# Expert rows cut into four column quarters and transposed by VectorE; expert weights in 4 KB runs

## The reference, cut to what matters

```
u = rms_norm(x, norm2_g) * (1 + sc2) + sh2
gate = two experts of one group of four, for each token, weights summing to 1
for e in 16 experts:  y += gate[:, e] * ((silu(u @ w1[e]) * (u @ w3[e])) @ w2[e])
x = x + g2 * y
```

## Time and profile before

| | us |
|---|---|
| median of 3 runs | 792.46 (792.24 to 792.88) |
| the profiled execution | 785.36 |
| its span, first to last instruction | 783.4 |
| TensorE busy | 627.1 (80%) |
| VectorE busy | 324.8 (41%) |
| ScalarE busy | 248.4 (32%) |
| mean TensorE clock granted | 0.915 |

### The profile page before, as it was taken

The page is one execution under the profiler, slowest core; times in us unless marked ns, Lnnn a source line. Parts: engine busy times, 40 slices in busy tenths (PEclk is TensorE's granted clock), DMA queues, the critical chain, the costliest instruction groups (busy, mean ns, idle before and its releaser), DMA issues.

```text
span 783.4 us, 15541 instructions
## 1 busy us (share of the span) xinstructions
PE 627.1 (80%) x6206; PEld 377.8 (48%) x6210; DVE 324.8 (41%) x917; ACT 248.4 (32%) x605; POOL 78.1 (10%) x118
## 2 busy tenths in 40 slices
PE   0389999977688889779988059989999999999940
PEld 0354465565355566554448035555555555555520
DVE  2824326523177797962352412222222222222215
ACT  2010100104255575851141023334433344433410
POOL 4010000007100000000000400011101111101122
PEclk9869999988889999999995579999999999999985
DMA  8894743343299300019016446999999999999228
GB/s 293 331 346 165 267 161 145 124 130 96 96 344 220 120 1 1 2 41 387 2 60 262 182 160 224 366 366 364 374 365 362 370 366 368 373 363 361 86 57 298
DMA packets 78108, 176.25 MB, mean 225 GB/s; under 512 B 9202, under 2 KB 24122, under 8 KB 75002
## 3 DMA queue, kind: packets, MB, share of 16 engines
q1 hardware_dynamic: 65328, 152.90, 55.7%
q0 software_dynamic: 8384, 13.97, 5.3%
q10 hardware_dynamic: 4364, 8.94, 3.6%
HBM read 155.02 MB, written 20.71 MB: 224 GB/s over the span
## 4 chain that ended last, share of the span: by engine, by line
PE 26%; DMA 23%; DVE 2%; issue 2%; POOL 2%; ACTq 0%; ACT 0%; POOLq 0%
DMA featT<-expert_rows 21%; PE score L1451 9%; PE score L1371 7%; PE bank L1441 3%; PE score L1460 3%; PE score L1411 2%; DMA pool_sb<-expert_rows,idx 1%; POOL expert_rows L727 1%; POOL pool_sb L747 1%; DMA expert_rows<-pool_sb,idx 1%; DMA expert_rows<-featT 1%; PE bank L1466 0%; ACTq L623 0%; PE bank L1403 0%; PE bank L1319 0%
## 5 line engine op out<-in xcount | busy, mean ns | idle before, releaser
L1451 PE MATMUL score<-pool_sb,featT 128*32 128x256 f32 x2688 | 162.6, 386 | 20.0 <-DMA featT<-expert_rows 11.3
L1451 PEld LDWEIGHTS score<-pool_sb,featT 128*32 128x32 f32 x2688 | 86.6, 111 | 82.1 <-DMA featT<-expert_rows 27.1
L1199 PE MATMUL bank<-pool_sb,featT 128*128 128x512 f32 (+2 forms) x320 | 113.7, 518 | 2.9 <-DVE pool_sb L804 1.9
L1128 DVE TENSOR_TENSOR featT<-featT,score 128x128 f32<-128x128 f32 x42 | 12.1, 288 | 184.2 <-ACT featT L634 184.2
L1199 PEld LDWEIGHTS bank<-pool_sb,featT 128*128 128x128 f32 x320 | 61.4, 193 | 54.9 <-issue 49.0
L1460 PE MATMUL score<-pool_sb,featT 128*32 128x256 f32 x1344 | 82.3, 386 | 0.4 <-ACT featT L639 0.4
L628 ACT ACTIVATE featT<-bank,mod_col 128x32 f32<-128x32 f32 x129 | 39.4, 375 | 61.4 <-PE bank L1441 61.4
L777 DVE SCALAR_TENSOR_TENSOR pool_sb<-pool_sb,cond 128x2048 f32<-128x2048 f32 x24 | 56.3, 2348 | 3.3 <-DMA pool_sb<-in_ada_b 1.7
L1118 DVE TENSOR_SCALAR featT<-bank,mod_col 128x32 f32<-128x32 f32 x215 | 51.0, 303 | 15.1 <-PE bank L1441 15.1
L735 POOL DMA_DIRECT2D expert_rows<-featT x42 | 29.2, 695 | 277.6 <-DVE featT L1124 264.0
L1371 PE MATMUL score<-pool_sb,featT 128*128 128x512 f32 x128 | 55.6, 594 | 0.0
(11 more groups left out here) (232 smaller groups left out, 648.3 us busy)
## 6 DMA issues: line engine op xcount, KB each, us to landing
pool_sb<-in_moe_w SPq DMA_DIRECT2D x48, 2048.0 KB, 22.1
pool_sb<-in_ada_w SPq DMA_DIRECT2D x24, 1024.0 KB, 5.0
expert_rows<-zeros_f SPq DMA_DIRECT2D x17, 512.0 KB, 6.7
featT<-expert_rows ACTq DMA_DIRECT2D x44, 128.0 KB, 5.4
expert_rows<-featT POOLq DMA_DIRECT2D x42, 128.0 KB, 7.1
pool_sb<-in_w_in SPq DMA_DIRECT2D x2, 2048.0 KB, 9.1
pool_sb<-in_w_out SPq DMA_DIRECT2D x4, 1024.0 KB, 16.9
x_sb<-in_x SPq DMA_DIRECT2D x1, 2048.0 KB, 7.9
```

What stands on the lines that cost most here:

```text
L1199: m = nc.tensor.matmul(banks[4 + i][:, 0:n], featT[:, k, i * P:(i + 1) * P], w_stage[:, g % 3, k, 0:n], start=(k == 0), stop=(k == KD - 1))
L1451: mm = nc.tensor.matmul(banks[0][h * BT:(h + 1) * BT, 0:2 * HB], xgT[:, k, :], exp_w13[slot][:, :, k, h * HB:(h + 1) * HB], start=(k == 0) ...
```

## The change

- **Rows.** A block is loaded as 4 x 32 quarters of 1 KB, quarter h into partitions 32h to 32h + 31, into two buffers in turn (`xg[n]`), three blocks ahead. VectorE multiplies by `scale2_part` and adds `shift2_part` (both new, held in quarters as the gate is), which gives `xm`, and transposes that in squares of 32 x 32 into `xgT` in one instruction that reads every eighth element. The transposes of TensorE and the eight evictions are gone.
- **Hidden rows.** `hmid` is transposed the same way by VectorE into `hT`; the turn on TensorE and the copy on ScalarE are gone. ScalarE keeps only the silu and the issue of the row loads.
- **Order.** `inner` no longer waits for row loads; it waits for `xgT` of its own block and for `hmid` of the block before.
- **Weights.** Input row p x 8 + k (for w2, p x 4 + k) now lies in partition p, which fits the squares. Each matrix comes in four DMAs with runs of 4 KB per partition, 16 KB (w2 too) apart from one partition to the next.
- **Ahead of the stage.** TensorE makes shift, gate and scale of the second norm in quarters (4 matmuls of 32 x 256 more at the second group, 8 of these in place of 2 of 128 x 512 at the third); VectorE copies them; four small DMAs of `norm2_g` are added at the start.

```diff
@@ sp
-                sp.dma_start(chunk_of(e % 3, m, DE // P if m == 2 else KD),
-                             MOE_W[m][0, e].rearrange("(k p) n -> p k n", p=P)).then_inc(done, 16)
+                rows = DE // P if m == 2 else KD
+                to, of = chunk_of(e % 3, m, rows), MOE_W[m][0, e].rearrange("(p k) n -> p k n", p=P)
+                for q in range(4):
+                    part = slice(q * rows // 4, (q + 1) * rows // 4)
+                    sp.dma_start(to[:, part, :], of[:, part, :]).then_inc(done, 16)
@@ act
+            def xg_load(g, n):
+                act.dma_start(xg[n], xs[bass.ds(g * BT, BT), :].rearrange("r (h n) -> h r n", h=NT)).then_inc(s_xg[n], 16)
+
+            def block_of_rows(g, n):
+                act.wait_ge(m_sc, g + 2)
+                xg_load(g + 3, 1 - n)
                 act.wait_ge(m_h1, g + 1)
                 nc.scalar.activation(silu, banks[0][:, 0:HB], ACT.Silu).then_inc(m_si, 1)
-                act.wait_ge(m_xt, g + 2)
-                xg_load(g + 2)
-                xg_T(g + 1)
-                act.wait_ge(m_ht, g + 1)
-                nc.scalar.activation(hT, banks[6][:, 0:P], ACT.Copy).then_inc(m_hT, 1)
@@ dve
+                                nc.vector.tensor_copy(shift2_part[:], banks[3][:, 0:DN])
...
-                                for h in range(NT):
-                                    at0 = (h * DN) % 512
-                                    nc.vector.tensor_copy(gate2_part[h * BT:(h + 1) * BT, :],
-                                                          banks[h * DN // 512][h * BT:(h + 1) * BT, at0:at0 + DN])
+                                nc.vector.tensor_copy(gate2_part[:], banks[0][:, 0:DN])
+                                dve.wait_ge(s_n2, 16 * NT)
+                                nc.vector.scalar_tensor_tensor(out=scale2_part[:], in0=banks[1][:, 0:DN], scalar=1.0, in1=scale2_part[:],
+                                                               op0=ALU.add, op1=ALU.mult)
...
+            def rows_in(g, n):
+                dve.wait_ge(s_xg[n], g * 8 + (16 if n == 0 else 8))
+                if not (isinstance(g, int) and g == 0):
+                    dve.wait_ge(m_xT, g)
+                nc.vector.tensor_tensor(xm, xg[n], scale2_part[:], ALU.mult).then_inc(m_sc, 1)
+                dve.wait_ge(m_sc, g + 1)
+                nc.vector.tensor_tensor(xm, xm, shift2_part[:], ALU.add).then_inc(m_mod, 1)
+
             def xg_T(g):
+                dve.wait_ge(m_mod, g + 1)
+                nc.vector.transpose(xgT, xm.rearrange("p (r k) -> p k r", k=KD)).then_inc(m_xT, 1)
+
+            def hmid_T(g):
+                dve.wait_ge(m_h, g + 1)
+                nc.vector.transpose(hT, hmid.rearrange("p (r k) -> p k r", k=NT)).then_inc(m_hT, 1)
...
+            def hidden(g):
+                dve.wait_ge(m_h1, g + 1)
+                xg_T(g + 1)
                 dve.wait_ge(m_si, g + 1)
+                if not (isinstance(g, int) and g == 0):
+                    dve.wait_ge(m_hT, g)
                 nc.vector.tensor_tensor(hmid, silu, banks[0][:, HB:2 * HB], ALU.mult).then_inc(m_h, 1)
+
+            def block_of_rows(g, n, y):
+                hidden(g)
+                dve.wait_ge(m_y, g)
+                hmid_T(g)
+                rows_out(y)
+                rows_in(g + 2, n)
@@ pe
+            def inner(slot, g):
+                pe.wait_ge(m_xT, g + 1)
                 for k in range(KD):
-                    if k == KD - 1:
-                        pe.wait_ge(s_xg, g * 16 + 32)
...
             def stage_of(g, slot, slot_before, uses):
-                pe.wait_ge(e_w13[slot], uses * 32)
+                pe.wait_ge(e_w13[slot], uses * 128)
+                pe.wait_ge(m_h, g)
                 inner(slot, g)
-                xg_T()
-                pe.wait_ge(e_w2[slot], uses * 16)
+                pe.wait_ge(e_w2[slot], uses * 64)
                 outer(g - 1, slot_before)
-                inner_T(g)
```

More of the change, by code:

```diff
@@ L77, in decoder_layer @@
         gate2_part = sb("gate2_part", [P, DN])
+        scale2_part = sb("scale2_part", [P, DN])
+        shift2_part = sb("shift2_part", [P, DN])
         gate1_row = sb("gate1_row", [P, D])
@@ L179, in decoder_layer, with blk_view @@
         blkbuf = featT[:, :, :].rearrange("p k n -> p (k n)")
[L180 to L186, removed]
+        blk_at = [0]
+        def blk_view(n):
+            blk_at[0] += n
+            return blkbuf[:, blk_at[0] - n:blk_at[0]]
+        xg = [blk_view(DN) for _ in range(2)]
+        xm = blk_view(DN)
+        xgT = blk_view(DN).rearrange("p (k r) -> p k r", r=BT)
+        silu = blk_view(HB)
+        hmid = blk_view(HB)
+        hT = blk_view(HB).rearrange("p (k r) -> p k r", r=BT)
+        y_sb = [blk_view(DN) for _ in range(2)]
+        y_last = [blk_view(DN) for _ in range(2)]
         yab = ring[:, :, 0:TT * D].rearrange("p b (i n) -> p b i n", i=TT)
@@ L316, in decoder_layer @@
         s_scat = sem("s_scat")
-        s_xg = sem("s_xg")
+        s_n2 = sem("s_n2")
+        s_xg = [sem(f"s_xg{n}") for n in range(2)]
+        m_mod = sem("m_mod")
+        m_sc = sem("m_sc")
         m_h1 = sem("m_h1")
@@ L320, in decoder_layer @@
         m_h = sem("m_h")
[L321 to L324, removed]
+        m_xT = sem("m_xT")
         m_hT = sem("m_hT")
@@ L380, in _ @@
                 sp.dma_start(vrow[28:32, b * DH:(b + 1) * DH], beta_swa[0, half].rearrange("(i d) -> i d", d=DH)).then_inc(s_small, 16)
+            for h in range(NT):
+                sp.dma_start(scale2_part[h * BT:(h + 1) * BT, :], norm2_g[0:1, h * DN:(h + 1) * DN].broadcast_to([BT, DN])).then_inc(s_n2, 16)
             for n, pos in enumerate((cmp_pos_k, cmp_pos_v)):
@@ L435, in _ @@
             load_matrix(2, 2)
-            sp.wait_ge(s_xg, 32)
+            sp.wait_ge(s_xg[0], 16)
+            sp.wait_ge(s_xg[1], 16)
             load_matrix(2, 0)
@@ L1136, in _ @@
             for g in range(1, 3):
-                block_of_rows(g)
-                rows_out(y_sb[(g - 1) % 2], g)
+                block_of_rows(g, g % 2, y_sb[(g - 1) % 2])
             with dve.Fori(1, pairs - 1) as m:
[L1140 to L1144, removed]
-                rows_out(y_sb[1], m * 2 + 2)
-            block_of_rows(pairs * 2 - 1)
-            last = dve.value_load(block_start[0:1, NE + 2:NE + 3], min_val=MIN_BLOCKS * NE - 1, max_val=MAXB)
-            rows_out(y_last[0], last)
-            rows_out(y_last[1], last + 1)
+                for n in range(2):
+                    hidden(m * 2 + 1 + n)
+                    dve.wait_ge(m_y, m * 2 + 1 + n)
+                    hmid_T(m * 2 + 1 + n)
+                    dve.wait_ge(s_ys[n], m * 16)
+                    rows_out(y_sb[n])
+                    rows_in(m * 2 + 3 + n, 1 - n)
+            last = dve.value_load(block_start[0:1, NE + 2:NE + 3], min_val=MIN_BLOCKS * NE - 1, max_val=MAXB)
+            hidden(last)
+            dve.wait_ge(m_y, last)
+            hmid_T(last)
+            rows_out(y_last[0])
+            dve.wait_ge(m_y, last + 1)
+            rows_out(y_last[1])
             for i in range(TT):
@@ L1211, in _, with quarters @@
                     row, col = (0, 1024) if g == 2 else (1024, 0)
-                    for h in range(2):
-                        nc.tensor.matmul(banks[h][:], ones[:], acc[:, b, row + h * 512:row + (h + 1) * 512], start=True, stop=True)
+                    def quarters(to, at0):
+                        for h in range(NT):
+                            nc.tensor.matmul(to[h * BT:(h + 1) * BT, 0:DN], ones[:, 0:BT], acc[:, b, at0 + h * DN:at0 + (h + 1) * DN],
+                                             start=True, stop=True)
+                    if g == 2:
+                        for h in range(2):
+                            nc.tensor.matmul(banks[h][:], ones[:], acc[:, b, row + h * 512:row + (h + 1) * 512], start=True, stop=True)
+                        quarters(banks[3], col)
+                    else:
+                        quarters(banks[0], row)
+                        quarters(banks[1], col)
                     for k in range(8):
@@ L1436, in _ @@
             m.then_inc(r_rank, 1)
-            def xg_T():
+            def inner(slot, g):
+                pe.wait_ge(m_xT, g + 1)
                 for k in range(KD):
-                    at0 = (k % 5) * BT
-                    m = nc.tensor.transpose(banks[4 + k // 5][:, at0:at0 + BT], xg[:, k * P:(k + 1) * P], ident[0:BT, 0:BT])
-                m.then_inc(m_xt, 1)
-            def inner(slot, g):
-                pe.wait_ge(m_xa, g + 1)
-                pe.wait_ge(m_xv, g + 1)
-                for k in range(KD):
-                    if k == KD - 1:
-                        pe.wait_ge(s_xg, g * 16 + 32)
                     for h in range(NT):
@@ L1480, in expert @@
                     stage_of(g, slot, slot, uses)
[L1482 to L1484 removed]
+            pe.wait_ge(e_w13[0], 128)
             inner(0, 0)
[L1486 to L1487 removed]
             pe.wait_ge(t_gs, 1)
```

52 lines of the change are left out of this document (17 added, 35 removed).

## The result

The changed kernel takes **801.66 us** (median of 4 runs, 799.78 to 804.19) against 792.35 (787.88 to 792.88, 4 runs) for the kernel before, run beside it: 1.0132 times as long, 95% interval 1.0084 to 1.018 (all ratios here are worked out over all the runs, so that they differ a little from the quotient of the medians). The forecast was 762.5 us, with a range up to 785. The profiled execution took 804.19 us.

What follows compares the result with a forecast made beforehand. The loop through one row buffer was taken as the bound, with the weights next. 785.36 - 29.1 - 0.9 = 755.4 us for the profiled execution; 30.0 off the median gave 762.5 us, range 754 to 785.

Steps and rivals of the forecast that it cites:

- the row load: In the block loop: a load, wanted two blocks on, lands in 7.1 us like the store; hidden, with cover to 10.3 us.
- the rows bind again: Rival, block loop: four times as many pieces queue, loads land in about 12.8 us, block near 6.85, 785.5 us; chance 0.12 (rows or VectorE).
- The signs of being wrong that came: Set beforehand: engine time per MB not falling, a block inside an expert over 6.3 us, or TensorE waiting on VectorE.
- Block of TensorE: In the expert stage: inner of 3.66 us and outer of 1.93 us remain, 5.6 us a block, hiding VectorE's new work.
- VectorE's transposes: In each block: 0.56 us for the 128 x 256 transpose and 0.35 in VectorE's sum of 2.5 us, under 5.6.
- Weights at 6.12 us a matrix: Weight stream of the stage: 4 KB runs at 42.3 us per MB save 0.32 us a matrix, from 6.44 to 6.12.
- the first rival: Weight stream: longer runs buy nothing, a matrix stays at 6.44 us, 773.0 us in all; chance 0.13.
- the slower rival: Weight stream: 16 KB spacing costs more than the runs save; at 50 us per MB, 7.13 us a matrix, 799.0 us; chance 0.09.
- Start of the stream: Start of the stage: the third inner frees slot 0, so the weight stream starts at 473.5 and not at 476.21.
- The 0.9 us forecast as gain there: Ahead of the stage: third group 1.8 us less, second group 0.9 us more, sum -0.9 us, bounds +0.9 and -1.8.
- End of the last outer: End of the stage: TensorE waits last for the 33rd matrix at 675.5, then needs 49.5 us: 725.0, 29.1 before 754.1.

Runs made afterwards that it cites:

- c_q4: The changed kernel with each row load as four DMAs, one for each column quarter, instead of one; 760.93 us, ratio 0.9625 to the kernel before.
- f_few: `c_q4` plus, every second block behind the silu, an unread load of 32 rows of `x` in one DMA, quarters first; 798.09 us.
- c_q4_kp1: `c_q4` with the weights loaded as before the change (one DMA a matrix, 2 KB runs); 766.06 us, ratio 0.9701 to the kernel before.
- b_pk4: The kernel before with weights loaded as in the changed kernel (four DMAs, 4 KB runs); 786.14 us, ratio 0.9972.
- b_four: The kernel before with each matrix in four DMAs, same placement and runs; 789.39 us, ratio 0.9984.
- d_b_pre: The kernel before with only the change's part ahead of the stage (quarters of shift, gate, scale, their copies, four small DMAs); 789.71 us against 791.97.
- f_all: As `f_few`, but the unread load's DRAM side is rows first with quarters merged, still one DMA; 766.98 us, ratio 0.9698 to the kernel before.

## Why the prediction was wrong, point by point

- **The step that failed is the row load.** "The store, which already moves quarters of 1 KB, in 7.1, at most 9.1. I take 7.1: hidden." The store and the load have the same pattern, but the store is issued by GpSimd and the load by ScalarE. After the change the store still lands in 7.3 us, and a load is taken 12.7 us after its issue, with VectorE waiting for it. The pieces were compared, not the number of engines that carry them, and even the pieces were not alike: the stores moved in packets of 4 KB. The size of the pieces is not what failed, for `c_q4` has them at 1 KB too and lands in 5.3. The change's DRAM side begins with `h`, size 4, and the load went to 4 engines.
- The Trainium skill ("DMA: Bandwidth & Descriptors", Why a DMA increments its semaphore by 16 and not by 1) has the rule: a DMA is divided among k engines, the largest k up to 16 that divides the slowest dimension, above 1, of both sides; and GpSimd's descriptors give some direct copies all 16 on this chip. The packet counts agree for ScalarE (132 and 36, against 48 and 192). For GpSimd's store they can't tell: it has 16 small packets under the same leading 4, but by the same section DMAs issued there report from all 16 engines whatever their shape. For it speaks that it lands in 7.3 us as before, and that `c_q4`, with this same store, has no lagging engines. I had drawn on this page for its bandwidth and did not hold this rule against the new pattern: it gives the cause that the runs then showed and that none of my rivals named.
- **What the step cost.** Its rival, "the rows bind again", had a landing of 12.8 us, and that it came so near is luck: its reason, four times as many pieces, is refuted by `c_q4`. It gave 785.5 us, since it let the weights flow at 6.12 us a matrix. They took (761 - 478) / 39 = 7.3 us to the last piece. Four engines carry all row loads beside their sixteenth each of every matrix, and a matrix is in when its slowest engine is; the estimate from the shares (7.2 us) and the tail fit this. 1.1 to 1.2 us more on 39 matrices is 44 to 45 us, a little over the 40.7 us between the changed kernel and `c_q4`. `f_few` shows a slowed stream at 31 us with less on the four engines. What the late rows add of their own is smaller: TensorE waits 9.8 us for VectorE's `hmid` (L1148), not at all in `c_q4`, but 48.9 us for weights against 24.5. An exact split was not measured.
- **The signs of being wrong that came.** Engine time per MB did not fall, 0.829 x 960 / 17.33 = 45.9 us from 600 to 660, and near the end inner follows inner after 752.31 - 744.75 = 7.56 us, over the 6.3 set, 2.18 of it waiting for VectorE.
- **Block of TensorE**, 5.6 us: 5.18 where nothing is late, for inner and outer overlap by 0.2 us each. A little high.
- **VectorE's transposes**, 0.56 and 0.35 us: 0.65 and 0.41 (page of the changed kernel, mean ns):

```profile
L1133 DVE STREAM_TRANSPOSE featT<-featT 128x256 f32<-128x256 f32 x43 | 27.9, 648 | 93.8 <-PE score L1486 93.2
L1137 DVE STREAM_TRANSPOSE featT<-featT 128x128 f32<-128x128 f32 x42 | 17.3, 412 | 56.4 <-PE score L1495 55.4
```

- **Weights at 6.12 us a matrix**: 6.10 in `c_q4`. The 4 KB runs are worth 5.1 us there (766.06 - 760.93) where the first rival had 10.5: the price of the old form falls from 45.2 to 0.925 x 2880 / 61.47 = 43.3 us per MB once the loop is gone (`c_q4_kp1`, 520 to 700: 61.47 MB at 92.5%). Why it falls was not asked. The 358 GB/s a core of the Trainium skill ("DMA: Bandwidth & Descriptors", Bandwidth), which the prediction did not follow, do not bind here: `c_q4` moves 391. The section ties that figure to two cores of a pair streaming at once, a condition that the prediction left out, and here one core runs.
- **Spacing of 16 KB**, the slower rival: no cost, 42.8 us per MB in `b_pk4`.
- **Start of the stream** at 473.5: 478.1 in the changed kernel. 3.7 us of it come from before the stage (first row load issued at 456.70 against 452.98). That is the spread between executions: `b_four`, whose part ahead is the old one, issues it at 458.83. The 0.9 us forecast as gain there are not seen, and `d_b_pre` could not tell them from none. **End of the last outer** at 725.0: 728.75 + 1.93 = 730.7 in `c_q4`, 5.7 us late. Its last wait for weights, the one for the 33rd matrix, ends at 681.12 and not at 675.5, and from there it takes 49.6 us, where the forecast had 49.5: the blocks are shorter than 5.6, but the first outer takes 3.4 us at a lower clock instead of 1.9.

```profile
681.12 3.38 PE L1496 MATMUL score<-pool_sb,featT 128*32 128x256 f32 x32 [2.36 <-DMA pool_sb<-in_moe_w]
...
728.75 1.93 PE L1496 MATMUL score<-pool_sb,featT 128*32 128x256 f32 x32 [0.92 <-DVE featT L1141]
```

So the sum was right for a kernel that differs from the changed one by one line, 762.5 forecast against 760.93 measured, and wrong for the one in hand. That it is right to 1.6 us is in part luck. For the profiled execution the sum gave 755.4 us, and that of `c_q4` took 761.26: the step from there to the median, 7.1 us, covered the late start and the rest.

## What to carry to other kernels

When a DMA's pattern is changed, look at the outermost size on both sides before its pieces: a rearrange that put a 4 in front put the whole transfer on 4 engines when ScalarE issued it. GpSimd's store with the same 4 in front showed no loss, and no run here tries SyncE. Such a load hurt twice, by landing late and by holding up the stream of weights beside it. What it takes from the stream can be estimated beforehand: its share of 16 engines times four, on the four engines that every matrix has to wait for. The cure was one DMA for each leading index (`c_q4`); `f_all` keeps one DMA and merges the sizes instead, `"r (h n) -> (r h) n"`, which puts the quarters into other partitions. The sign of it is in the packet count (data pieces plus 4 instead of 16) and in a tail of the big stream at a fraction of the engines, not in the DMA slices, which stay at 9.

## What the runs showed of the hardware that was not expected

- A 128 KB load on 4 engines, once for every second block, made the kernel 31 us longer than the same load on all. Its 128 packets of 1 KB took 52 ns each in `f_few` (500 to 690 us), so that one load is 1.7 us on each of the four engines and some 20 of them are 33 us, against 8 us on sixteen: an estimate, and it gives most of the difference.
- Weight pieces of 8 KB are the best of 4, 8 and 16 KB (760.93, 756.04, 779.55 us): engine time per MB no longer falls beyond 8 KB, while the small row pieces beside them land in 5.3, 6.2 and 7.8 us.
- ScalarE loads its table for the silu (1.28 us) in 21 of 42 blocks; before it did so in all 42. It comes in every second block, at 736.91 and 750.18 us, between late rows and the silu, and not at 743.82 and 757.72.
